# One core: Z records dealt unevenly over the points, one weight load moved ahead of a wait, and the mLSTM output projection as four block pairs

## The chip, the cores and the metric

The kernel runs on one core of one Trainium2 chip. The metric is the device time of one execution in microseconds. The engines are TensorE (PE; its weight loads, PEld, overlap its matmuls), VectorE (DVE), ScalarE (ACT), GpSimd (POOL) and SyncE (SP), which issues most transfers. Each engine works in order. Semaphores tie the programs together: `x.then_inc(s, n)` counts up when x ends, and `wait_ge(s, n)` holds an engine until the count is there.

## What is computed

One decoder layer over 1024 tokens of width 1024, in fp32. Two mixers read one projection of the normed input and are merged by gates:

```python
mod = jax.nn.silu(c) @ w_ada[l] + b_ada[l]
h = rms_norm(x, g_norm[l]) * (1.0 + scale) + shift
proj = h @ w_in[l]
xa, va, oa, za, ia, fa, qa, ka, vat, zb, ga, gb = jnp.split(proj, split_at, axis=-1)
xc = jax.nn.silu(causal_depthwise_conv(xa, w_conv[l], b_conv[l]))
h_m = mlstm_chunkwise(q_m, k_m, v_m, ia + b_igate[l], fa + b_fgate[l])   # 4 heads of 256
h_m = jax.nn.sigmoid(oa) * h_m
h_m = rms_norm(h_m, g_mlstm_head[l]) + skip_mlstm[l] * xc
y_m = (h_m * jax.nn.silu(za)) @ w_out_mlstm[l]                          # 1024 x 1024
...                                    # 3 groups x 4 heads of dilated window attention
o_a = jnp.sum(wts[..., None] * jnp.stack(outs, axis=0), axis=0)
y_a = (o_a * jax.nn.silu(zb)) @ w_out_attn[l]                           # 512 x 1024
merged = jax.nn.sigmoid(ga) * y_m + jax.nn.sigmoid(gb) * y_a
x = x + gate * (merged @ w_out[l])
return rms_norm(x, g_final)
```

Shapes and names are shortened here; the code above is the reference cut to its core.

## The kernel before

**Precision.** Every large product is formed in three passes on PE: an operand is split into a high part (an fp32r copy, mostly made by ACT) and a low part (the rest, by POOL or DVE as a subtraction), and `three_pass` issues high·high, low·high and high·low (lines L592, L593, L594). One such matmul of 128x512 is called a record below.

**Stages.** Setup; then 28 *block pairs*, in which four 512x512 blocks of the input projection are had from seven products instead of eight (`ORDER = (5, 1, 2, 4, 6, 7, 3)`, 12 records each), with sums of the factor blocks made once by DVE and sums of weight blocks made for each pair; then four mixed stages, one for each head; then `merge`; then `finish`.

**A head's stage.** PE forms the rest of the head's projection, and last its Z (two chunks ZA and ZA+1, two halves each, 24 records a half: 96 records). The Z records are dealt out over 24 *points*, four at each; between them `mixing(u)` issues what the two mixers have at point u: an mLSTM chunk (scores, numerator, state, turn) and attention tasks (scores, transposes of the exponentials, p·v). These small matmuls wait for DVE, ACT and POOL. ACT copies a finished half out of its bank (`keep`), makes high parts of the next weights (`next_high`), and at points 17 to 21 takes the roots for the norms. After the last point `turn_output` (L1366) transposes the normed and gated head. `turn_stats` on SP stores the head's gated rows `um` (`mlstm_branch`), loads the softmax statistics `ct`, waits for the group weights `cw` (semaphore `cw_done`), stores them and spreads them over partitions. SP loads the ring of weights `wraw` with `load`; the fourth load of the next head stands behind these waits.

**merge.** `first_pairs` projects the gates of output tiles 0 and 1 (8 units of 24 records; the weights of the second four are made high by `pair_high` on ACT and low by POOL in line L1248). Meanwhile SP loads all eight `um` tiles back, and DVE combines the last head's attention groups (`scale_two`, `join_two`, `join_third`, `gate_attn`). Then `branch` forms, for each of eight tiles m of 128 output channels, the mLSTM part (16 x 24 = 384 records in all) and the attention part (192 records), with weights loaded and split for each. DVE's `merge_tile(m)` multiplies both by their gates and adds them into `mg`; ACT stores the tile to DRAM (`mg_d`) as soon as it is merged. Tiles 2 to 7 do mLSTM then attention, alternately; the last two units of PE's work are mLSTM tile 7 and attention tile 7.

**finish.** POOL waits until tiles 0 to 6 are in DRAM, loads 128 tokens of all of them back (`wraw<-merged`), splits them (L2178, L2181), and only then can PE form the first output tile; tile 7 is taken from SBUF. PE forms 8 token tiles of the output projection, DVE and ACT the final norm.

The waits which set this order around the merge, in code:

```python
pool.wait_ge(mg_out, 16 * KT)                      # finish: tiles 0 to 6 stored
pool.dma_start(mr[:, b, 0:KT - 1], rows[:, 0:KT - 1, b * P:(b + 1) * P]).then_inc(m_in[b], 16)
pe.wait_ge(m_part, 1)                              # finish: first high and low parts are there
act.wait_ge(merged_half, 4 * m + 4)                # merge: tile m is merged
act.dma_start(mg_d[m], mg[:]).then_inc(mg_out, 16)
```

## Time and profile before

| | before |
|---|---|
| runs | 1370.96 us median of 3 (1369.63 to 1371.36) |
| profiled execution, its time | 1371.11 us |
| its span | 1369.3 us |
| mean granted clock of PE | 0.999 of full speed |
| PE busy | 1345.7 us (98%) |
| DVE, ACT, POOL busy | 855.3, 580.1, 463.0 us (62%, 42%, 34%) |
| chain that ended last | PE 87%, DVE 6%, ACT 3%, DMA 2% |

The span runs from the first to the last instruction on the engines; the time of the execution is 1.8 us more. Matmuls are pipelined, so a matmul's listed duration (389 ns for a record) is more than its share of PE's time: eight records that follow each other start 0.227 us apart. The stages in the trace, by their first matmuls: blocks to about 610, heads at 610, 734.3, 856, 976.5, merge 1097.8, its branch products 1141.4, output 1273.45, last matmul about 1363.

### The profile page before, as it was taken

How to read it: one execution, taken by the hardware profiler on the slowest of the kernel's cores; microseconds unless marked ns; L12 is line 12 of the kernel's file. 1: busy time of each engine (PE TensorE's matmuls, PEld its weight loads, DVE VectorE, ACT ScalarE, POOL GpSimd, SP SyncE). 2: the span in 40 equal slices, each digit the busy share in tenths (PEclk: the TensorE clock that was granted, in tenths of full speed). 3: DMA queues.
4: the chain of work that ended last, by engine and by line, in shares of the span. 5: the costliest groups of instructions: out<-in, count | busy, mean ns of one | idle time of the engine just before them, and what ended most of it. 6: DMA issues, size and time to landing. Idle time of an engine off the chain costs nothing.

```text
span 1369.3 us, 17469 instructions
## 1 busy us (share of the span) xinstructions
PE 1345.7 (98%) x6453; PEld 1126.9 (82%) x6453; DVE 855.3 (62%) x1472; ACT 580.1 (42%) x1016; POOL 463.0 (34%) x298
## 2 busy tenths in 40 slices
PE   8999999999999999999999999999999999999998
PEld 6888888888888888888898788889878887888886
DVE  7988766573745444535368757866875766434586
ACT  7663353343444344332545446354545534111122
POOL 0096555554545555543002200210120022222551
PEclk9999999999999999999999999999999999999999
DMA  8522323323234343337231841553172165453543
GB/s 316 196 82 95 132 99 123 123 93 115 101 123 139 123 143 134 139 112 228 73 83 48 231 93 32 161 148 94 48 227 67 33 241 205 128 187 140 173 138 108
DMA packets 65454, 180.52 MB, mean 132 GB/s; under 512 B 22001, under 2 KB 22129, under 8 KB 63318
## 3 DMA queue, kind: packets, MB, share of 16 engines
q1 hardware_dynamic: 61082, 166.64, 36.9%
q10 hardware_dynamic: 3168, 8.70, 1.9%
q0 software_dynamic: 1120, 4.06, 1.0%
q8 instruction: 52, 0.85, 0.3%
q14 instruction: 32, 0.26, 0.1%
HBM read 132.49 MB, written 46.89 MB: 131 GB/s over the span
## 4 chain that ended last, share of the span: by engine, by line
PE 87%; DVE 6%; ACT 3%; DMA 2%; issue 1%; SPq 0%; POOL 0%; ACTq 0%; DVEq 0%
PE banks L592 23%; PE banks L594 23%; PE banks L593 23%; PE banks L1265 4%; PE banks L1390 2%; PE banks L1400 2%; PE banks L1350 2%; PE banks L1356 2%; DMA wraw<-in_w_all 1%; PE banks L1339 1%; PE banks L1348 1%; PE banks L1409 1%; PE banks L584 1%; PE banks L556 1%; PE banks L1378 1%
## 5 line engine op out<-in xcount | busy, mean ns | idle before, releaser
L1248 POOL TENSOR_TENSOR wlo<-wraw,whi 128x1024 fp32r<-128x1024 f32 x28 | 72.1, 2575 | 436.5 <-ACT whi L1468 411.1
L718 POOL TENSOR_TENSOR wlo<-w_sum,whi 128x512 fp32r<-128x512 f32 x112 | 165.2, 1477 | 137.4 <-ACT whi L843 137.4
L592 PE MATMUL banks<-t_hi,whi 128*128 128x512 f32 x448 | 174.3, 389 | 0.0
L593 PE MATMUL banks<-t_lo,whi 128*128 128x512 f32 x448 | 174.3, 389 | 0.0
L594 PE MATMUL banks<-t_hi,wlo 128*128 128x512 f32 x448 | 174.3, 389 | 0.0
L989 DVE TENSOR_TENSOR c_sum<-c_sum,banks 128x512 f32<-128x512 f32 x196 | 134.4, 686 | 44.7 <-PE banks L594 30.6
L592 PE MATMUL banks<-h_hi,whi 128*128 128x512 f32 x416 | 162.0, 389 | 0.0
L594 PE MATMUL banks<-h_hi,wlo 128*128 128x512 f32 x416 | 161.9, 389 | 0.0
L593 PE MATMUL banks<-h_lo,whi 128*128 128x512 f32 x416 | 161.8, 389 | 0.0
L843 ACT ACTIVATE whi<-w_sum 128x512 fp32r<-128x512 f32 x112 | 70.5, 630 | 165.5 <-PE banks L594 100.7
L592 PE MATMUL banks<-whi,h_hi 128*128 128x512 f32 x256 | 100.2, 391 | 1.4 <-POOL wlo L1248 1.4
L594 PE MATMUL banks<-whi,h_lo 128*128 128x512 f32 x256 | 99.7, 389 | 0.0
L593 PE MATMUL banks<-wlo,h_hi 128*128 128x512 f32 x256 | 99.6, 389 | 0.0
L593 PEld LDWEIGHTS banks<-t_lo,whi 128*128 128x128 f32 x448 | 84.1, 188 | 17.5
L594 PEld LDWEIGHTS banks<-t_hi,wlo 128*128 128x128 f32 x448 | 84.1, 188 | 17.4
L592 PEld LDWEIGHTS banks<-t_hi,whi 128*128 128x128 f32 x448 | 84.1, 188 | 17.4
L592 PEld LDWEIGHTS banks<-h_hi,whi 128*128 128x128 f32 x416 | 78.1, 188 | 16.3 <-POOL wlo L1248 0.2
L594 PEld LDWEIGHTS banks<-h_hi,wlo 128*128 128x128 f32 x416 | 78.1, 188 | 16.3
L593 PEld LDWEIGHTS banks<-h_lo,whi 128*128 128x128 f32 x416 | 78.1, 188 | 16.2
L865 ACT ACTIVATE fin<-c_sum 128x1024 f32<-128x1024 f32 x56 | 79.4, 1467 | 2.4 <-DMA chunk_decay_rows<-wlast 2.3
L718 POOL TENSOR_TENSOR wlo<-wraw,whi 128x512 fp32r<-128x512 f32 x42 | 63.0, 1507 | 48.8 <-ACT whi L843 48.8
L718 POOL TENSOR_TENSOR wlo<-raw,whi 128x512 fp32r<-128x512 f32 x42 | 58.5, 1402 | 51.3 <-ACT whi L843 51.3
(374 smaller groups left out, 2904.8 us busy)
## 6 DMA issues: line engine op xcount, KB each, us to landing
wraw<-in_w_all SPq DMA_DIRECT2D x72, 512.0 KB, 4.3
raw<-in_w_all SPq DMA_DIRECT2D x28, 512.0 KB, 4.4
queries_keys<-fin SPq DMA_DIRECT2D x12, 1024.0 KB, 4.0
qa<-queries_keys SPq DMA_DIRECT2D x12, 768.0 KB, 13.7
s_wada<-in_w_ada_cols SPq DMA_DIRECT2D x16, 512.0 KB, 8.2
attn_values<-fin SPq DMA_DIRECT2D x6, 1024.0 KB, 4.0
tn<-attn_values SPq DMA_DIRECT2D x12, 512.0 KB, 10.1
sig_c<-merge_gates SPq DMA_DIRECT2D x6, 1024.0 KB, 6.4
```

The source lines that it names most:

```text
L592: t_.matmul(out, w_hi, x_hi, start=first, stop=False)
L593: t_.matmul(out, w_hi, x_lo, start=False, stop=False)
L594: return t_.matmul(out, w_lo, x_hi, start=False, stop=last)
L718: nc.gpsimd.tensor_tensor(wlo4[:, o % 4, :], source(r, j), whi4[:, o % 4, :].bitcast(F32), subtract).then_inc(s_split, 1)
L843: A(whi4[:, o % 4, :], source(r, j), ACT.Copy).then_inc(s_high, 1)
L865: A(fin[r % 2][:, j, :].rearrange("p (r u) -> p r u", r=d), c_sum[:, r % 2, j, :].rearrange("p (u r) -> p r u", r=d), ACT.Sigmoid if r < Q ...
L989: v.tensor_tensor(out, x, bank(r, j), ALU.add).then_inc(part_added, 1)
L1248: nc.gpsimd.tensor_tensor(to, wraw[:, q % 2, :], hi.bitcast(F32), ALU.subtract).then_inc(w_split, 1)
L1265: mm = t_.matmul(ps[:, h, :], w[:, to, k * P:(k + 1) * P], x[:, k, h * HALF:(h + 1) * HALF], start=(e == 0), stop=(e == 3 * KT - 1))
L1350: mm = t_.matmul(M2[:, 0:DH + 1], qm[:, d, c * P:(c + 1) * P], cst[:, d, :], start=(d == 0), stop=(d == 1))
L1356: mm = t_.matmul((M1, M2)[d][:, 0:DH + 1], kw[:, c % 2, d * P:(d + 1) * P], v1[:, c, 0:DH + 1], start=True, stop=True)
L1390: mm = t_.matmul(A0[:, u * 2 * P:u * 2 * P + b * P], qa[:, g % 2, 0, t * P:(t + 1) * P], qa[:, g % 2, 1, (t + 1 - b) * P:(t + 1) * P], sta ...
```

## The change

It has three parts.

1. **Heads.** The 96 Z records of a head are dealt out over the 24 points by the table `SIZES`: 4, 4, 6, 7, then twelve times 3, three times 4, then 7, 4, 4, 6, 6. ACT's `keep` and `next_high` move with the records: the second half is now finished at point 12 instead of 11, the third at point 19 (after the point's mixing) instead of 17.
2. **Weight load.** For heads 1 to 3 the fourth load of the ring is issued in `turn_stats` of the head before, after `ct` and before the wait for `cw_done`.
3. **Branch.** The mLSTM part of the merge is formed as four more block pairs, r = 28 to 31: 7 products of 12 records each, 336 instead of 384. The factor blocks are quarters of `um` (128x4x512 a piece); DVE makes four differences and seven low parts of them, ACT seven high parts. For each pair DVE makes four sums of weight blocks, ACT and POOL split seven, ACT keeps the first product, and DVE adds the others (`join`, seven additions) into `umo`, then multiplies two tiles by their gates. All eight attention tiles (8 x 24 records) follow after the four pairs. The rows of `um` for it are loaded by `gather_branch` on SP, ahead of `ct`; the last head's two come straight from SBUF. `weigh_groups` and `group_exp` of head 3 move from the end of the heads into the merge's programs. Gates come in halves, and the output weights in another order (`OUT_ORDER`). The wait of `finish` for the stored tiles 0 to 6 stays.

```diff
+    RECORDS = 3 * KT
+    SIZES = (4, 4, 6, 7) + 12 * (3,) + 3 * (4,) + (7, 4, 4, 6, 6)
+    ENDS = list(itertools.accumulate(SIZES))
+    POINTS = len(SIZES)
...
+        def gather_branch():
+            um_raw, tile_in = T["um_raw"], T["tile_in"]
+            sp.wait_ge(out_turned, 4 * HEADS)
+            for q in range(2):
+                sp.wait_ge(um_out[q], 16 * HEADS)
+            for k in range(KH):
+                sp.dma_start(um_raw[:, k, :], um_d[k // 2, k % 2]).then_inc(tile_in[k], 16)
+            for q in range(2):
+                sp.wait_ge(um_done, 2 * HEADS - 1 + q)
+                sp.dma_start(um_raw[:, KT - 2 + q, :], xc[:, q, :]).then_inc(tile_in[KT - 2 + q], 16)
...
-            for q in range(2):
+            if i == HEADS - 1:
+                gather_branch()
+            for q in range(2) if i < HEADS - 1 else ():
                 sp.wait_ge(um_done, i * 2 + q + 1)
                 sp.dma_start(um_d[i, q], xc[:, q, :]).then_inc(um_out[q], 16)
             sp.wait_ge(stat_out, (i + 1) * 16 * sum(STATS))
             sp.dma_start(ct[:].rearrange("p g c w -> p g (c w)"), stat_d.rearrange("g (p c) w -> p g (c w)", c=NCH)).then_inc(ct_in, 16)
+            for k in range(KH, KT - 2) if i == HEADS - 1 else ():
+                sp.dma_start(T["um_raw"][:, k, :], um_d[k // 2, k % 2]).then_inc(T["tile_in"][k], 16)
+            if i + 1 < HEADS:
+                load(HEAD0 + (i + 1) * CHUNKS + AHEAD)
             sp.wait_ge(cw_done, i + 1)
             sp.dma_start(coef_d.rearrange("g (p c) -> p g c", c=NCH), cw[:, 2]).then_inc(coef_out, 16)
...
-                load(HEAD0 + i * CHUNKS + p + AHEAD)
+                if p or not i:
+                    load(HEAD0 + i * CHUNKS + p + AHEAD)
...
+            for u in range(POINTS):
+                for record in range(ENDS[u] - SIZES[u], ENDS[u]):
+                    project(record)
+                if u == 1:
+                    head_q()
+                if (i, u) == (0, 2):
+                    pe.wait_ge(decays_in, 32)
+                    t_.transpose(M1[:, 0:P], gr[:], ident[:]).then_inc(hc_turned, 1)
+                mixing(u)
...
+            for u in range(POINTS):
+                if u == formed_at(ZA, 0):
+                    keep(ZA, 0)
+                if u == formed_at(ZA, 1):
+                    keep(ZA, 1)
+                    next_high(ZA + 2)
+                if u == formed_at(ZA + 1, 1):
+                    keep(ZA + 1, 1)
+                    next_high(ZA + 3)
+                if u == 1:
+                    exp_table()
...
+                    keep(ZA + 1, 0)
+                if u == TURN - 2:
...
+        load_pair(PAIRS)
         sp.wait_ge(T["ua_done"], 2 * HEADS + 1)
         sp.dma_start(ua_d[HEADS - 1], T["mixing"]["szb"][:]).then_inc(ua_out, 16)
+        load_pair(PAIRS + 1)
...
+        for r in BRANCH_PAIRS:
+            for j in ORDER:
+                o = at_product(r, j)
+                pool.wait_ge(s_high, o + 1)
+                nc.gpsimd.tensor_tensor(wlo4[:, o % 4, :], source(r, j), whi4[:, o % 4, :].bitcast(F32), ALU.subtract).then_inc(s_split, 1)
...
+        def product(r, j):
+            o = at_product(r, j)
+            bank_free(o)
+            pe.wait_ge(s_split, o + 1)
+            if r == PAIRS:
+                pe.wait_ge(t_lo_done, low_count(j))
+            hi, lo = factors[j]
+            for k in range(KH):
+                cols = slice(k * P, (k + 1) * P)
+                mm = three_pass(t_, bank(r, j), whi4[:, o % 4, cols], wlo4[:, o % 4, cols], hi[:, k, :], lo[:, k, :],
+                                k == 0, k == KH - 1)
+            mm.then_inc(gprod, 1)
...
+        for r in BRANCH_PAIRS:
+            for j in ORDER:
+                product(r, j)
+        for m in range(KT):
+            attn_branch(m)
...
+        def weight_high(o):
+            r, j = o // PRODUCTS, ORDER[o % PRODUCTS]
+            if o < TOTAL + 4:
+                act.wait_ge(proj, PROJ0 + 4 * PLAIN - (1 if o < TOTAL + 2 else 0))
+            else:
+                act.wait_ge(gprod, o - 3)
+            if j in plain_at:
+                act.wait_ge(pair_in[r % 2], 32 * (r // 2 + 1))
+            else:
+                act.wait_ge(s_added, made(r, j))
+            A(whi4[:, o % 4, :], source(r, j), ACT.Copy).then_inc(s_high, 1)
...
         act.sem_inc(mg_out, 16)
+        branch_high(up_left_hi, up_left[0], range(KH))
+        T["shared"]["group_exp"](HEADS - 1)
         first_sigmoid(0, 0, 1)
         first_sigmoid(0, 1, 1)
+        sum_high(5)
         pair_high(0)
         first_sigmoid(0, 0, 0)
         pair_high(1)
         first_sigmoid(0, 1, 0)
+        branch_high(low_left_hi, low_left[0], range(KH, KT))
         first_sigmoid(1, 0, 1)
-        split_high(0)
-        split_high(1)
         first_sigmoid(1, 1, 1)
-        split_high(2)
-        split_high(3)
-        branch_high(0)
+        weight_high(TOTAL)
+        weight_high(TOTAL + 1)
         first_sigmoid(1, 0, 0)
-        split_high(4)
-        split_high(5)
-        branch_high(1)
+        act.wait_ge(ua_out, 16 * HEADS + 16)
+        sum_high(6)
+        sum_high(4)
         first_sigmoid(1, 1, 0)
-        for k in range(EARLY, KB):
-            split_high(k)
-        branch_high(2)
-        for k in range(2):
-            out_high(k)
+        weight_high(TOTAL + 2)
+        weight_high(TOTAL + 3)
+        for o in range(TOTAL, WITH_BRANCH):
+            r, j = o // PRODUCTS, ORDER[o % PRODUCTS]
+            if j == 1:
+                keep_first(r)
+            if o + 4 < WITH_BRANCH:
+                weight_high(o + 4)
+            if o == TOTAL:
+                sum_high(7)
+            if o == TOTAL + 1:
+                branch_high(low_right_hi, low_right[0], range(KH, KT))
+        attn_weights_high(0)
+        for k in range(HEADS):
+            attn_high(k)
+        attn_weights_high(1)
         for m in range(KT):
-            for r in (2 * m + 3, 2 * m + 4):
-                if r < 2 * KT:
-                    branch_high(r)
-            act.wait_ge(merged_half, 4 * m + 4)
-            act.dma_start(mg_d[m], mg[:]).then_inc(mg_out, 16)
             if m + 2 < KT:
-                out_high(m + 2)
+                attn_weights_high(m + 2)
+            act.wait_ge(merged_half, merged(m, 4))
+            if m == KT - 1:
+                act.wait_ge(mg_out, 16 * KT)
+            act.dma_start(mg_d[m], umo[:, m, :]).then_inc(mg_out, 16)
+            if m < len(WO_AT):
+                for e in WO_AT[m]:
+                    out_high(e)
...
+        def difference(j, x, y, first=None):
+            if first is not None:
+                dve.wait_ge(t_raw, raw_count(first))
+            v.tensor_tensor(bt_raw[j], x, y, ALU.subtract).then_inc(t_raw, 1)
...
+        def low(j, raw_):
+            hi, lo = factors[j]
+            dve.wait_ge(t_hi_done, high_count(j))
+            v.tensor_tensor(lo, raw_, f(hi), ALU.subtract).then_inc(t_lo_done, 1)
...
+        def weight_sums(r):
+            dve.wait_ge(pair_in[r % 2], 32 * (r // 2 + 1))
+            dve.wait_ge(s_split, PRODUCTS * r)
+            combine(5, quarter(r, 1, 0), quarter(r, 1, 1), ALU.add)
+            combine(7, quarter(r, 0, 0), quarter(r, 1, 0), ALU.subtract)
+            dve.wait_ge(s_added, made(r, 5))
+            combine(6, sum_at[5], quarter(r, 0, 0), ALU.subtract)
+            dve.wait_ge(s_added, made(r, 6))
+            combine(3, quarter(r, 0, 1), sum_at[6], ALU.subtract)
...
         dve.sem_inc(T["added"], 4)
-        T["shared"]["scale_two"](HEADS - 1)
-        T["shared"]["join_two"](HEADS - 1)
-        T["shared"]["join_third"](HEADS - 1)
-        T["shared"]["gate_attn"](HEADS - 1)
-        for k in range(KB):
-            split_low(k)
-        for k in range(2):
-            out_low(k)
+        branch_rows(range(KH))
+        dve.wait_ge(pv_kept, 12 * HEADS + 1)
+        difference(5, up_right, up_left[0])
+        T["shared"]["weigh_groups"](HEADS - 1)
+        low(1, up_left[0])
+        branch_rows(range(KH, KT))
+        difference(6, low_right[0], bt_raw[5], 5)
+        low(5, bt_raw[5])
+        for part in ("scale_two", "join_two", "join_third", "gate_attn"):
+            T["shared"][part](HEADS - 1)
+        dve.wait_ge(T["ua_done"], 2 * HEADS + 1)
+        weight_sums(PAIRS)
+        difference(4, low_left[0], bt_raw[6], 6)
+        low(2, low_left[0])
+        low(4, bt_raw[4])
+        low(6, bt_raw[6])
+        difference(7, low_right[0], up_right)
+        low(7, bt_raw[7])
+        low(3, low_right[0])
+        for r in BRANCH_PAIRS:
+            if r + 1 in BRANCH_PAIRS:
+                weight_sums(r + 1)
+            else:
+                for k in range(HEADS):
+                    attn_low(k)
+            join(r)
+            for j in range(2):
+                gate(2 * (r - PAIRS) + j)
         for m in range(KT):
             merge_tile(m)
-            if m + 2 < KT:
-                out_low(m + 2)
+            if m < len(WO_AT):
+                for e in WO_AT[m]:
+                    out_low(e)
```

**PE, the last points of head 3**, before: `pT,vt` is p·v of an attention task, `ident,sm` a transpose of exponentials, L1265 a Z record.

```order
L1390 MATMUL banks<-qa 128x128 x2
L1400 MATMUL banks<-pT,vt 128x128 x2
L1409 MATMUL banks<-ident,sm 128x128 x2
L1265 MATMUL banks<-h_lo,whi 128x512
L1265 MATMUL banks<-h_hi,wlo 128x512
L1265 MATMUL banks<-h_hi,whi 128x512
L1265 MATMUL banks<-h_lo,whi 128x512
L1400 MATMUL banks<-pT,vt 128x128 x2
L1409 MATMUL banks<-ident,sm 128x128 x2
```

PE, the same place in the changed kernel (L1308 is a Z record):

```order
L1433 MATMUL banks<-qa 128x128 x2
L1443 MATMUL banks<-pT,vt 128x128 x2
L1452 MATMUL banks<-ident,sm 128x128 x2
L1308 MATMUL banks<-h_hi,whi 128x512
L1308 MATMUL banks<-h_lo,whi 128x512
L1308 MATMUL banks<-h_hi,wlo 128x512
L1308 MATMUL banks<-h_hi,whi 128x512
L1308 MATMUL banks<-h_lo,whi 128x512
L1308 MATMUL banks<-h_hi,wlo 128x512
L1308 MATMUL banks<-h_hi,whi 128x512
L1443 MATMUL banks<-pT,vt 128x128 x2
L1452 MATMUL banks<-ident,sm 128x128 x2
```

Between one transpose of exponentials and the next attention product there are now seven records at point 19, where there were four.

**SP, from the last store of statistics to the merge**, before: `mlstm_branch` is the DRAM home of `um`, `ct` the statistics, `group_weights` the spread weights.

```order
L1176 DMA softmax_stats<-st 512x1x2
L1149 DMA wraw<-in_w_all 128x1024 [waits w_split]
L1182 DMA mlstm_branch<-xc 128x1024 [waits um_done] x2
L1184 DMA ct<-softmax_stats 128x3x16 [waits stat_out]
L1186 DMA group_weights<-cw 128x3x8 [waits cw_done]
L1193 DMA qm<-group_weights 128x1024 [waits coef_out]
L1193 DMA qm<-group_weights 128x1024
L1193 DMA vt<-group_weights 128x1024 [waits pv_kept]
L1936 DMA um_lo_raw<-mlstm_branch 128x1024 [waits p_kept,pv_kept,masked,um_out0,out_used,um_out1,acc_out,early_out]
L1936 DMA um_lo_raw<-mlstm_branch 128x1024 x7
L1919 DMA wraw<-in_w_all 128x1024 [waits w_split] x2
```

SP, the same place in the changed kernel:

```order
L1173 DMA wraw<-in_w_all 128x1024 [waits w_split]
L1208 DMA um_lo_raw<-mlstm_branch 128x1024 [waits um_out1,um_out0,out_turned]
L1208 DMA um_lo_raw<-mlstm_branch 128x1024 x3
L1211 DMA um_lo_raw<-xc 128x1024 [waits um_done] x2
L1221 DMA ct<-softmax_stats 128x3x16 [waits stat_out]
L1223 DMA um_lo_raw<-mlstm_branch 128x1024 x2
L1227 DMA group_weights<-cw 128x3x8 [waits cw_done]
L1234 DMA qm<-group_weights 128x1024 [waits coef_out]
L1234 DMA qm<-group_weights 128x1024
L1234 DMA vt<-group_weights 128x1024 [waits pv_kept]
L1986 DMA wraw<-in_w_all 128x1024 [waits w_split,acc_out,early_out]
L1986 DMA wraw<-in_w_all 128x1024
```

The loads of `um` now stand ahead of `ct` and of the wait for `cw_done`; the weights of the first two block pairs follow behind the spreads, and `w_split` of the second gate pair stands before them.

**ACT, the start of the merge**, before: L2021 is a sigmoid of a finished gate unit, L2027 `pair_high`.

```order
L1545 ACT_TABLE_LOAD
L1545 ACTIVATE cw<-cw 128x24 [waits ct_arg]
L2021 ACT_TABLE_LOAD
L2021 ACTIVATE qa<-banks 128x512 [waits proj] x2
L2027 ACTIVATE whi<-wraw 128x1024 [waits w_in0,proj]
L2021 ACTIVATE qa<-banks 128x512 [waits proj]
L2027 ACTIVATE whi<-wraw 128x1024 [waits w_in1,proj]
L2021 ACTIVATE qa<-banks 128x512 [waits proj] x2
```

ACT, the same place in the changed kernel (L2143 the sigmoids, L2149 `pair_high`, L2155 and L2160 high parts of factor blocks):

```order
L2155 ACTIVATE up_left_hi<-um_lo_raw 128x2048 [waits tile_in2,tile_in3,tile_in1,tile_in0]
L1587 ACT_TABLE_LOAD
L1587 ACTIVATE cw<-cw 128x24 [waits ct_arg]
L2143 ACT_TABLE_LOAD
L2143 ACTIVATE qa<-banks 128x512 [waits proj] x2
L2160 ACTIVATE bt_hi<-bt_lo_raw 128x2048 [waits t_raw]
L2149 ACTIVATE whi<-wraw 128x1024 [waits w_in0,proj]
L2143 ACTIVATE qa<-banks 128x512 [waits proj]
L2149 ACTIVATE whi<-wraw 128x1024 [waits w_in1,proj]
L2143 ACTIVATE qa<-banks 128x512 [waits proj]
L2155 ACTIVATE low_left_hi<-um_lo_raw 128x2048 [waits tile_in6,tile_in7,tile_in5,tile_in4]
L2143 ACTIVATE qa<-banks 128x512 [waits proj] x2
```

Ahead of the first `pair_high` there now stand the high part of a block of `um`, the exponential of the group weights with its table, and the high part of the first difference.

## Rows read from the trace of the kernel before

**Rows 1.** Waits of PE: line that waited, releaser, total us, times, longest

```profile
PE banks L1366 <- DVE og L1719: 2.2, 4, 0.6
...
PE banks L1400 <- ACT ew L1565: 1.8, 4, 0.4
PE banks L592 <- POOL wlo L1248: 1.4, 2, 1.0
...
PE banks L592 <- DVE um_lo L2085: 0.8, 2, 0.6
```

**Rows 2.** Windows by stage: length, busy us and count of each engine, clock, DMA share

```profile
1097.80:1141.40 43.60, 43.60 (x195) 35.99 (x194) 28.84 (x29) 16.86 (x21) 11.17 (x4) 1.00 0.63 230
...
1273.45:1369.30 95.85, 89.28 (x413) 74.03 (x411) 66.96 (x111) 20.59 (x51) 37.95 (x23) 0.98 0.39 127
```

**Rows 3.** Timeline of SP and ACT around head 3's fourth weight load

```profile
998.60 1.19 SPq L1149 DMA_DIRECT2D wraw<-in_w_all  x2
...
1006.44 1.06 ACT L1468 ACTIVATE whi<-wraw 128x1024 fp32r<-128x1024 f32 x1 [3.09 <-DMA wraw<-in_w_all]
```

**Rows 4.** Timeline of ACT and PE at point 4 of head 3

```profile
1037.18 0.19 ACT L1570 ACTIVATION_READ_ACCUMULATOR sm<-sm,nm 128x1 f32 x1
...
1037.46 0.51 PE L1409 MATMUL banks<-ident,sm 128*128 128x128 f32 x3
```

**Rows 5.** Page, transfers: KB each, median us to landing; SP's timeline, start of merge

```profile
wraw<-in_w_all SPq DMA_DIRECT2D x72, 512.0 KB, 4.3
...
1100.84 0.35 SPq L1149 DMA_DIRECT2D wraw<-in_w_all  x1
```

**Rows 6.** Timeline of ACT, POOL and DVE in the merge's gate units

```profile
1108.24 1.28 ACT L2021 ACT_TABLE_LOAD   x1
...
1114.45 1.06 ACT L2027 ACTIVATE whi<-wraw 128x1024 fp32r<-128x1024 f32 x1 [3.83 <-PE banks L594]
...
1115.59 2.39 POOL L1248 TENSOR_TENSOR wlo<-wraw,whi 128x1024 fp32r<-128x1024 f32 x1 [14.77 <-ACT whi L2027]
...
1119.47 3.25 DVE L1787 TENSOR_TENSOR num<-num,qm 128x1024 f32<-128x1024 f32 x2 [10.17 <-DMA vt<-group_weights]
...
1132.14 2.35 DVE L2085 TENSOR_TENSOR um_lo<-um_lo_raw,um_hi_a 128x1024 fp32r<-128x1024 f32 x2
```

**Rows 7.** Timeline of DVE and POOL in setup, and of POOL in the blocks

```profile
57.50 2.35 DVE L919 TENSOR_TENSOR t_lo_raw<-s_xnT 128x1024 f32<-128x1024 f32 x2
59.88 4.58 DVE L919 TENSOR_TENSOR t_lo_raw<-s_xnT,t_lo_raw 128x1024 f32<-128x1024 f32 x2
...
59.83 2.41 POOL L723 TENSOR_TENSOR wlo<-wraw,whi 128x1024 fp32r<-128x1024 f32 x1 [56.88 <-ACT whi L875]
...
299.49 1.29 POOL L718 TENSOR_TENSOR wlo<-w_sum,whi 128x512 fp32r<-128x512 f32 x1 [0.88 <-ACT whi L843]
```

**Rows 8.** Timeline of DVE, ACT and POOL from merged tile 6 to the output

```profile
1259.91 0.69 DVE L2108 TENSOR_TENSOR num<-num,sig_c 128x512 f32<-128x512 f32 x1
...
1260.63 15.58 ACTq L2074 DMA_DIRECT2D merged<-num  x2
...
1263.58 2.10 POOL L2187 DMA_DIRECT2D wraw<-merged  x2 [3.88 <-DMA merged<-num]
1268.23 1.67 POOL L2178 TENSOR_TENSOR m_first<-wraw,zero 128x896 fp32r<-128x896 f32 x1 [2.54 <-DMA wraw<-merged]
1269.98 2.13 POOL L2181 TENSOR_TENSOR m_first<-wraw,m_first 128x896 fp32r<-128x896 f32 x1
```

**Rows 9.** Windows after the last matmul and around PE's first dense work

```profile
1362.00:1365.00 3.00, 0.73 (x7) 0.52 (x5) 1.68 (x6) 0.71 (x3) 0.00 (x0) 1.00 0.00 0
...
1366.00:1369.30 3.30, 0.00 (x0) 0.00 (x0) 0.10 (x1) 0.33 (x1) 0.00 (x0) 0.50 0.42 159
10.80:14.00 3.20, 3.20 (x16) 3.20 (x16) 2.69 (x6) 1.93 (x2) 0.00 (x0) 1.00 1.01 412
14.00:15.60 1.60, 1.60 (x17) 1.60 (x16) 0.83 (x6) 1.28 (x4) 0.00 (x0) 1.00 1.02 412
```

435 lines of the change are left out of this document (257 added, 178 removed).

## The prediction

> **What bounds the kernel now.** I read the page's busy table first: PE is busy 1345.7 of 1369.3 us at a clock of 0.999, so this kernel is the row of its matmuls and the few places where that row stops. The page gives both. Then the waits of PE [rows 1], which name those stops: four short ones ahead of L1366 (the turn of a head's output), four ahead of L1400 (p·v at point 18), two ahead of L592 for low weight parts, two for low parts of `um`. Then windows by stage [rows 2]: the gate units take 43.60 us for 192 records, so a record costs 43.60 / 192 = 0.227 us of PE, whatever its listed duration says. Then the timelines of the other engines at the places where the change puts work. There the reader is to ask what stands between two engines and how much PE work covers it.
>
> **What it removes.**
> 1. 48 records of the branch (384 to 336): 48 x 0.227 = -10.9 us. No other engine ends the stretch there, so PE's time goes in full.
> 2. The two waits for `um_lo`: -0.8 [rows 1]. Those tiles are gone; the new factor parts are priced below.
> 3. L1366: 2.2 us in 4 waits, 0.55 a head [rows 1]. The numerator whose normed value it waits for comes at point 18. From there to the turn there were 20 records (4 before each of points 19 to 23), now 7 + 4 + 4 + 6 + 6 = 27. Seven more are 1.6 us, over 0.55: -2.2.
> 4. L1400: 1.8 us in 4, 0.45 each [rows 1]. It waits for ACT's weight L1565, queued behind the norm's square. The 7 records ahead of point 19 in place of 4 are 0.68 us of cover against 0.45: -1.8.
> 5. The low weights L1248: 1.4 us in 2 waits, 1.0 the longest [rows 1]. Of head 3, SP issues the load of this slot at 998.60, behind the group weights and their spreads, and ACT stands 3.09 us idle for it before its high part at 1006.44 [rows 3]. Issued ahead of the `cw_done` wait it is earlier by several us: -1.4.
>
> Sum of what goes: 10.9 + 0.8 + 2.2 + 1.8 + 1.4 = 17.1 us.
>
> **What the heads pay.** The twelve points with three records have one record less between a task's scores and the use of its exponentials. At point 4 of head 3 ACT's exponential ends at 1037.18 + 0.19 = 1037.37 and PE takes it at 1037.46 [rows 4]: 0.09 us in hand, and a record is 0.227, so a new wait of about 0.14 us there. Most other points have more in hand; I take 0.25 a head, +1.0. Bounds: nothing, if DVE's earlier start gives it back, and all 12 points exposed in 4 heads, 48 x 0.227 = +10.9.
>
> **The first pair's factors: the gate units.** Today the high part of the second gate weights starts at 1114.45 and ends at 1115.51, and POOL splits it from 1115.59 to 1117.98 [rows 6]. PE needs it after four units, at 1097.80 + 4 x 24 x 0.227 = 1119.6: 1.6 us in hand. With the wait at L1366 gone PE comes there at 1119.0. In the new ACT program five things stand ahead: the high part of the first four `um` tiles, the exponential with its table, the sigmoid's table, two sigmoids, and the high part of the first difference, which DVE must form first. When do the tiles land? SP is through with the last ring load at 1100.84; that load and four tiles are 5 x 0.52 = 2.6 MB, at the 412 GB/s which the queues move in a full stretch [rows 9] 6.4 us, plus what one such load takes beyond its own 1.3 us of transfer, 4.3 - 1.3 = 3.0 [rows 5]: 1110.2. DVE's difference is two 128x1024 pieces, 2.35 us [rows 7], to 1112.6; the group weights then take 0.5. ACT's parts are four tables or copies: after 1113.1 a sigmoid table of 1.28 [rows 6] and the exponential 0.2, two sigmoids 1.1, a copy of 128x2048 2.0 (two of the 1.06 copies, less their overlap) and `pair_high` 1.06: 1118.8. The exponential's own table, 1.28, can load only after the first copy, 1110.2 + 2.0 + 1.3 = 1113.5, which moves this to 1119.1. POOL's 2.39 makes it 1121.5 against 1119.0: **+2.4** us of wait. It is us for us with the landing: at the best case (tiles 2.4 us sooner) nothing.
>
> **The first pair's factors: the products.** DVE's attention chain runs from 1119.47 to 1132.2 today, when the spreads have landed [rows 6]. The statistics now stand behind six tiles, so I move it by 4 to 5 us, to about 1136. Behind it stand four weight sums (0.7 each) and, until product 3, two differences and five low parts, each 2.35 us. A product is 12 records, 2.72 us, and five of the seven products of this pair (2, 4, 6, 7, 3) need one or two such DVE steps: 2, 4, 6 and 3 one, 7 two, and one more difference ahead of 2. Alone DVE would just hold: 2.35 against 2.72. But POOL splits a weight block in each product, 1.29 us alone [rows 7], and the two do not run beside each other here: from 59.88 two DVE subtractions of 2.35 took 4.58 us, with a POOL subtraction of 2.41 lying at 59.83 [rows 7]; 2.35 + 2.41 = 4.76. So a product in this pair takes 2.35 + 1.29 = 3.64 us, 0.92 more than 2.72. Over six products 5.5 us. Some splits fall in DVE's own waits for ACT, so I take **+4.0**; bounds 0 and 5.5. The Trainium skill (page "SBUF — State Buffer", section "SBUF: two separate sides") says that a VectorE operation with two inputs in SBUF and a GpSimd operation that reads SBUF hold a shared port pair in turn, the loser blocked for the whole instruction. By that rule it would be the full 5.5, by the naive reading of separate engines nothing. Rows 7 agree with the rule.
>
> In pairs 29 to 31 DVE has sums 2.8, joins 4.8 (banks) and gates 2.4 us in 19.0, POOL 9.0; that fits, as in the 28 pairs before, where PE has no wait for either.
>
> **The output: what becomes visible.** Follow merged tile 6 today [rows 8]: DVE's last addition ends at 1260.60, ACT issues the store at 1260.63, POOL is released at 1263.58, its load is back at 1268.23, its two subtractions (1.67, 2.13) end at 1272.11. 11.5 us, and the output starts at 1273.45 [rows 2]: it all lay under mLSTM tile 7 and attention tile 7, 72 records or 16.3 us. In the new order only attention tile 7 follows attention tile 6: 24 records, 5.44 us. Tile 6 is merged 4 x 0.69 less the overlap with its own second half, about 1.7 us, after its last record; so 5.44 - 1.7 = 3.7 us before PE's end, and the chain needs 11.5: **+7.8** us in which PE has nothing to do. Bounds: 7.0, and 10 if DVE is late with tile 6 (eight output-weight low parts stand between the tiles).
>
> **The clock.** PE idles 7.8 us. The last matmuls are over by about 1363; the granted clock is 1.00 in 1362 to 1365 and 0.50, the 1.2 GHz level, from 1366 on [rows 9]. So it will be down when the output starts. No row shows a rise of the granted clock. The nearest is PE's pace in its first dense work: 16 matmuls in the 3.2 us from 10.8 and 17 of the same in the next 1.6 us, though the clock column says 1.00 for both [rows 9]. If that is what a rise looks like, half of 3.2 us is lost: **+1.6** (bounds 0, if the clock stays up, and 3.2, twice the stretch). The Trainium skill ("TensorE: Matmul & The Clock Gate", table "The two states you'll see") has the same two levels, 1.2 GHz after idling and 2.4 GHz after sustained work. The trace agrees for the fall; that the chip starts low is its reading of the first stretch, which the column doesn't show.
>
> **Sum**, against the profiled execution's own 1371.1 us (span 1369.3 and 1.8 around it), which is 0.15 over the median of the three runs: 1371.1 - 17.1 + 1.0 + 2.4 + 4.0 + 7.8 + 1.6 = **1370.8 us**, the median's own size: no difference.
>
> **The rivals.**
> - *The factor steps keep ahead* (0.25). The tiles land 2.4 us sooner, as transfers of head 3 are out of the way, and POOL's splits fall into DVE's gaps: 1370.8 - 2.4 - 4.0 = 1364.4. For it: DVE is idle 10.17 us before 1119.47 [rows 6]. Against: rows 7.
> - *The output's chain is partly covered, or the clock stays up* (0.10). If only half of the 7.8 shows and the clock holds, 1370.8 - 3.9 - 1.6 = 1365.3. Against: nothing but one 5.44 us unit is left behind tile 6.
> - *Slower: the gather lands late* (0.15). `pair_high` is chained to the landing us for us. The 4.7 MB of all tiles, statistics and last load share the queues; if the first four tiles come 4 us later than 1110.2, the wait is 6.4 and the attention chain and everything behind it moves too: 1374.8. It decides (slower by over 0.2%) from 3 us late.
> - *Slower: short points exposed* (0.10). If the 48 shortened points each show their record, 1370.8 - 1.0 + 10.9 = 1380.7; a third of them is enough for slower. For it: 0.09 us in hand in rows 4. Against: one point of twelve was that tight.
> - *The heads' part does nothing* (0.05), since other waits end at the same time: 5.4 - 1.0 back, 1375.2.
> - My forecast as it stands, 1368.2 to 1373.7: 0.35.
>
> **How the numbers follow.** A measurement of this kernel tells apart about 0.2%, 2.7 us: faster is under 1368.2, slower over 1373.7. Faster: the first two rivals, 0.35. Same: 0.37, the forecast and 0.02 of mild cases of the rivals. Slower: 0.28. The range leaves out the exposed points and the far end of the first two: 1363.5 to 1376.0; the likeliest case's own range is 1368 to 1374.
>
> **What would show it.** In the profile after: no wait at L1366's and L1400's successors, and none for the low weights in the heads; a wait of 2 to 3 us of PE on POOL's low weights at the fifth gate unit; in the first branch pair waits of about 0.9 us on DVE's low parts, product by product, with POOL splits of over 1.5 us; then pairs without waits; an idle stretch of PE of 7 to 9 us before the first output matmul, ended by POOL's split; and 1.2 GHz in the 3 us after it. What would make it wrong: DVE late in the attention tiles, so that the idle stretch is over 10 us; or output weights that land after tile 4, so that ACT holds up the attention weights.

## The result: 1.5% slower

The changed kernel takes 1392.45 us (median of 4 runs, 1383.21 to 1395.48) against 1371.16 us before (4 runs): ratio 1.0146, 95% interval 1.0097 to 1.0194. The forecast was 1370.8, the range ended at 1376.0. Its profiled execution took 1393.01 us (span 1391.2), 21.9 more than that of before. The edges of the stages in the two traces, by their first matmuls, say where:

| stretch | before | after | difference | forecast |
|---|---|---|---|---|
| start to the first folded projection | 662.1 | 663.7 | +1.6 | 0 |
| four heads, to the last turn | 433.7 | 441.6 | +7.9 | -4.4 |
| last turn to the first output matmul | 177.6 | 187.3 | +9.6 | +2.5 |
| first output matmul to the end | 95.9 | 98.6 | +2.8 | +1.6 |

The folded projection is the first product of a head with `fold` as an operand, and a turn is the first matmul of L1366 (L1409 after). The first row is no part of the change, but it is part of the time: in setup, which has the same work in both kernels, the granted clock fell in this execution and not in that of before. The same window of both (length, busy us and count of PE, PEld, DVE, ACT, POOL, granted clock, DMA share, GB/s), first before, then after:

```profile
28.50:32.00 3.50, 3.50 (x21) 2.80 (x21) 3.36 (x7) 3.43 (x4) 0.00 (x0) 1.00 0.81 234
28.50:32.00 3.50, 3.50 (x14) 3.02 (x13) 3.42 (x7) 3.43 (x4) 0.00 (x0) 0.51 1.00 343
```

That is 3.4 us at half the clock, 1.7 us lost. The last stop of PE ahead of it was 0.5 us (at 26), in both kernels. Of the 14 profiled executions of this text nine have this fall and begin their first folded projection at 662.8 to 664.1, and five (before, e3, e4, e6 and e8) do not and begin it at 661.7 to 662.1.

The four runs of the changed kernel spread over 12 us, and the mean granted clock goes with them: 1383.21 us at 0.994, 1391.89 at 0.990, 1393.01 and 1395.48 at 0.986. What follows is read from the 1393.01 us, near the median; the shortest of the four shows that not all of the loss comes in every execution. The kernel before had medians of 1371.16, 1370.06, 1370.26 and 1370.36 us beside the result, e1 to e4, e5 to e8 and e9 to e12, so differences between runs of different sets are good to about 1 us.

PE's waits in the changed kernel, by line, releaser, total us, times, longest:

```profile
PE banks L614 <- POOL m_first L2407: 7.8, 1, 7.8
PE banks L1443 <- DVE pT L1810: 7.6, 4, 1.9
...
PE banks L614 <- POOL wlo L2060: 3.5, 1, 3.5
...
PE banks L614 <- POOL wlo L1290: 2.6, 1, 2.6
...
PE banks L614 <- POOL wlo L2056: 1.5, 2, 1.3
```

The waits of [rows 1] are gone, all four kinds, as forecast. New are: 7.8 ahead of the output (forecast 7.8), 2.6 at the gate units (2.4), 1.5 in the first pair under a name and more in pieces (below). And two that no sum had: 7.6 us at L1443 in four waits of 1.9, in the heads, and 3.5 at L2060, in the attention tiles.

**The wait in the heads.** ACT, DVE, POOL and PE in head 4 around point 12:

```profile
1073.09 0.57 ACT L1494 ACTIVATE cv<-banks 128x512 f32<-128x512 f32 x1
1073.57 1.04 ACT L1510 ACTIVATE whi<-wraw 128x1024 fp32r<-128x1024 f32 x1
1074.51 0.46 ACT L1578 ACTIVATE hin<-banks,hc 128x257 f32<-128x257 f32 x1
...
1074.69 2.37 POOL L1290 TENSOR_TENSOR wlo<-wraw,whi 128x1024 fp32r<-128x1024 f32 x1 [39.09 <-ACT whi L1510]
...
1075.01 0.43 DVE L1734 TENSOR_TENSOR hnb<-banks,hin 128x257 f32<-128x257 f32 x1 [2.32 <-ACT hin L1578]
...
1075.66 1.42 DVE L1741 SCALAR_TENSOR_TENSOR small<-hnb,hc,small 128x1 f32<-128x1 f32 x1
...
1078.52 0.62 DVE L1810 COPY pT<-banks 128x128 f32<-128x128 f32 x2
...
1079.19 1.02 PE L1443 MATMUL banks<-pT,vt 128*128 128x128 f32 x6 [1.90 <-DVE pT L1810]
```

ACT copies the finished half out of its bank (L1494) and makes the next weights high (L1510, 1.04 us) before the mLSTM's state term (L1578). DVE stands 2.32 us for that term (1.22 in e1 below, where the copies come later). Then an operation on one column, L1741, takes 1.42 us, and ends with POOL's split of those same weights (POOL is busy 1074.69 to 1077.06). In the kernel before, the same operation took 0.22 us all 32 times. The transposed exponentials (L1810) come last, and PE waits for them. So the two copies hold up PE in two ways: in ACT's own queue, and through the split that they release on POOL. Before the change, they stood at point 11, and PE's longest wait at p·v was 0.4 us [rows 1].

**And the clock falls.** Windows of the changed kernel, in one-microsecond steps behind that wait:

```profile
1079.00:1080.00 1.00, 0.81 (x6) 0.81 (x7) 1.00 (x4) 1.00 (x6) 0.00 (x0) 0.95 0.99 373
1080.00:1081.00 1.00, 1.00 (x6) 0.98 (x5) 0.62 (x3) 0.41 (x2) 0.00 (x0) 0.50 0.98 401
...
1082.00:1083.00 1.00, 1.00 (x4) 0.81 (x3) 0.00 (x0) 0.00 (x0) 0.00 (x0) 0.50 0.16 2
1083.00:1084.00 1.00, 1.00 (x5) 0.82 (x5) 0.00 (x0) 0.00 (x0) 0.00 (x0) 0.84 0.02 0
```

PE is up to full work again at 1079.2, and from 1079.9 to about 1083.3 it is granted 0.50, the 1.2 GHz level: 3.4 us at half the clock, 1.7 us lost. So a stop of 1.9 us costs about 3.6 here. It is so in all four heads of this execution. The sum closes: from folded projection to turn a head takes 73.0 us where it took 70.3, 2.7 more, which is 1.9 + 1.7 less the 0.95 of the two short waits that are gone.

**The merge's start**, where [rows 6] are of before: ACT, POOL and PE at the second gate weights:

```profile
1120.49 1.92 ACT L2155 ACTIVATE up_left_hi<-um_lo_raw 128x2048 fp32r<-128x2048 f32 x1 [11.45 <-DMA um_lo_raw<-mlstm_branch]
...
1128.29 1.06 ACT L2149 ACTIVATE whi<-wraw 128x1024 fp32r<-128x1024 f32 x1
...
1129.43 6.86 POOL L1290 TENSOR_TENSOR wlo<-wraw,whi 128x1024 fp32r<-128x1024 f32 x2 [18.86 <-ACT whi L2149]
...
1131.94 0.50 PE L614 MATMUL banks<-h_hi,whi 128*128 128x512 f32 x1 [2.64 <-POOL wlo L1290]
```

The first four tiles of `um` land at 1120.5, 9.9 us behind the last ring load (1110.59); 9.4 were forecast. ACT's high part of the gate weights ends at 1129.35 behind its queue, and PE stands 2.64 us.

**The attention tiles.** SP, ACT and PE at tile 5:

```profile
1257.65 0.33 SPq L2007 DMA_DIRECT2D gate<-merge_gates  x1
1258.02 0.43 SPq L1994 DMA_DIRECT2D wraw<-in_w_all  x1
...
1263.40 0.63 ACT L2183 ACTIVATE whi<-wraw 128x512 fp32r<-128x512 f32 x1 [3.33 <-DMA wraw<-in_w_all]
...
1265.43 0.80 PE L614 MATMUL banks<-ua_hi_a,whi 128*128 128x512 f32 x1 [3.50 <-POOL wlo L2060]
```

The weights of tile 5 are issued at 1258.02, directly behind a gate load (1257.65) that had to wait until tile 2 was merged, land 5.4 us later, and PE, done with tile 4 at 1261.9, waits 3.5 us. The clock follows here too, and stays at 0.50 until about 1271.0 (a mean of 0.90 over the second window is one microsecond at 0.50):

```profile
1265.00:1270.00 5.00, 4.57 (x11) 3.61 (x12) 3.80 (x5) 0.78 (x2) 0.37 (x1) 0.50 0.76 262
1270.00:1275.00 5.00, 5.00 (x21) 4.05 (x20) 3.45 (x5) 1.45 (x2) 1.29 (x1) 0.90 0.77 231
```

**The output.** POOL's load and subtractions, and the windows of the first output matmuls:

```profile
1283.74 2.10 POOL L2413 DMA_DIRECT2D wraw<-merged  x2 [5.65 <-DMA merged<-umo]
1288.70 1.67 POOL L2404 TENSOR_TENSOR m_first<-wraw,zero 128x896 fp32r<-128x896 f32 x1 [2.86 <-DMA wraw<-merged]
1290.45 2.07 POOL L2407 TENSOR_TENSOR m_first<-wraw,m_first 128x896 fp32r<-128x896 f32 x1
...
1285.00:1290.00 5.00, 0.00 (x0) 0.00 (x0) 1.23 (x2) 0.00 (x0) 2.14 (x2) 0.81 0.89 260
1290.00:1295.00 5.00, 2.43 (x6) 1.97 (x7) 0.00 (x0) 0.00 (x0) 3.43 (x6) 0.50 1.00 379
1295.00:1300.00 5.00, 5.00 (x17) 3.98 (x16) 0.00 (x0) 0.00 (x0) 4.68 (x5) 0.66 0.43 175
1300.00:1305.00 5.00, 5.00 (x20) 3.44 (x19) 2.12 (x3) 0.00 (x0) 0.78 (x1) 1.00 0.35 105
```

This is the chain of [rows 8], link by link, now in the open: load 1283.74, parts 1288.70 and 1290.45, first output matmul at 1292.57, where PE's last branch matmul ended at 1284.8. Tile 6 was merged 4.1 us before that (3.7 were forecast), and from there the chain took 11.8 us (11.5 before). The clock is at 0.50 until about 1298.3, 5.8 us after PE has resumed: half of that is 2.9 us, and the output stage is 2.8 us longer.

### The profile page after: what moved, and what is told of

It reads as the page before. It is cut to its first block, busy times and chain, and to the rows that moved or that the text cites. A ratio compares the mean times of both kernels' runs of the same rounds, so it can differ in the third digit from the quotient of the medians.

```text
span 1391.2 us, 17535 instructions
## 1 busy us (share of the span) xinstructions
PE 1350.2 (97%) x6405; PEld 1128.3 (81%) x6405; DVE 913.2 (66%) x1511; ACT 595.2 (43%) x1039; POOL 501.0 (36%) x318
## 4 chain that ended last, share of the span: by engine, by line
PE 79%; DVE 9%; ACT 4%; POOL 3%; DMA 3%; issue 1%; SPq 0%; ACTq 0%; DVEq 0%; POOLq 0%
PE banks L614 21%; PE banks L616 21%; PE banks L615 20%; PE banks L1308 5%; PE banks L1443 2%; POOL wlo L739 2%; PE banks L1433 2%; PE banks L1393 1%; PE banks L1399 1%; PE banks L1391 1%; PE banks L1452 1%; PE banks L578 1%; DMA wraw<-in_w_all 1%; DVE bt_lo L2259 1%; PE banks L1421 1%
## 5 line engine op out<-in xcount | busy, mean ns | idle before, releaser
L1290 POOL TENSOR_TENSOR wlo<-wraw,whi 128x1024 fp32r<-128x1024 f32 x28 | 75.0, 2681 | 440.6 <-ACT whi L1510 414.1
```

What stands on the lines that cost most here:

```text
L1290: nc.gpsimd.tensor_tensor(to, wraw[:, q % 2, :], hi.bitcast(F32), ALU.subtract).then_inc(w_split, 1)
```

## The experiments

Theory after the result: (1) in the heads it is ACT's two copies, moved from point 11 to point 12, and not the number of records; (2) a stop of PE of about 2 us or more can be followed by a fall of the clock, and that costs 1.7 to 2.9 us besides; (3) the attention wait is SP's order; (4) the output's wait is the round trip through DRAM. The rivals stand in the expectations. e1 serves as the base of e5 to e9, e11 and e12.

**e1, the copies behind point 12.**

```diff
-                if u == formed_at(ZA, 1):
-                    keep(ZA, 1)
-                    next_high(ZA + 2)
...
                 mixing(u)
+                if u == formed_at(ZA, 1):
+                    keep(ZA, 1)
+                    next_high(ZA + 2)
```

> The changed kernel, with ACT's keep of the second Z half and the copy of the next weights issued behind mixing(12) and not ahead of it. Theory: these two (0.57 and 1.04 us) hold up ACT's state term at point 12, DVE stands 2.3 us for it, PE 1.9 us for p transposed (L1443), four times, and each such stop lets PE's granted clock fall to 0.50 for some 4 us, about 1.7 us more. Then both go: 4 x 3.7 = 15 us less, about 1378 us, no window under 1.00 in the heads. Rival (three records in place of four are too little cover at any point, wherever ACT's copies stand): the four waits of 1.9 us stay, 1392 us.

Measured 1376.93 us (4 runs), 1.0054 of before (1.0039 to 1.0069), 15.5 less than the changed kernel. No wait at L1443 is left:

```profile
PE banks L614 <- POOL m_first L2407: 7.1, 1, 7.1
...
PE banks L614 <- POOL wlo L2060: 4.1, 2, 3.8
PE banks L614 <- POOL wlo L2056: 3.8, 1, 3.8
...
PE banks L614 <- POOL wlo L1290: 2.5, 1, 2.5
```

From the first folded projection to the last turn there are now 426.1 us, 7.7 less than before the change, where 4.4 were forecast. Of the 7.7, 4.9 us lie between folded projection and turn, in the part with the points, and 2.8 between a turn and the next folded projection, where part 2 works (e4's profile has 2.2 there). The edit moves the copies and with them POOL's split (L1741 takes at most 0.22 us in e1), so it does not tell ACT's queue and POOL's split apart.

**e2, even deal; e3, part 1 alone; e4, part 2 alone.** e2 is the changed kernel with four records at each point:

```diff
-    SIZES = (4, 4, 6, 7) + 12 * (3,) + 3 * (4,) + (7, 4, 4, 6, 6)
+    SIZES = 24 * (4,)
...
+                if u == formed_at(ZA + 1, 0):
+                    keep(ZA + 1, 0)
...
                 mixing(u)
-                if u == formed_at(ZA + 1, 0):
-                    keep(ZA + 1, 0)
```

> The changed kernel with four Z records at each point and ACT's keeps where the kernel before has them (part 1 undone; parts 2 and 3 stay). Theory: each head's stretch from its folded projection to its turn comes back from 73.0 to 70.3 us, so about 10 us less than the changed kernel, 1382 us, with the short waits at L1443 and at the turn (0.4 and 0.6 us a head) back. Rival (part 2 or 3 lengthens the heads): 1392 us.

e3 is the kernel before with the diff's hunks on `SIZES`, PE's and ACT's loops over the points. e4 is the kernel before with

```diff
+            if i + 1 < HEADS:
+                load(HEAD0 + (i + 1) * CHUNKS + AHEAD)
             sp.wait_ge(cw_done, i + 1)
...
-                load(HEAD0 + i * CHUNKS + p + AHEAD)
+                if p or not i:
+                    load(HEAD0 + i * CHUNKS + p + AHEAD)
```

> The kernel before with part 1 alone (table SIZES and ACT's keeps as in the change). Theory: the loss in the heads is part 1's own: 4 x 2.7 = 11 us more than before, about 1382 us, with the waits of 1.9 us at p.v and the clock at 0.50 behind each. Rival (it takes parts 2 or 3 to make it): within 3 us of 1371, or 4 us less as forecast.

> The kernel before with part 2 alone (fourth weight load ahead of the wait for cw_done). Forecast of the prediction: the two waits of PE on low weights L1248 (1.4 us) go, 1369.6 us; rival: the load was no cause, another wait takes their place, 1371 us.

| | median us | ratio to before, 95% |
|---|---|---|
| e2 | 1381.55 (4 runs) | 1.0084 (1.0068 to 1.0099) |
| e3 | 1376.77 (4 runs) | 1.0059 (1.0041 to 1.0077) |
| e4 | 1368.61 (10 runs) | 0.9990 (0.9980 to 0.9999) |

e2 met its number: part 1 as it was made costs 11 us beside an even deal. e3 has the four waits of 1.9 us, but is 5 us under its expectation, and its trace offers a reason. Windows of six microseconds behind the wait, first and second head of e3:

```profile
708.00:714.00 6.00, 5.34 (x25) 4.69 (x25) 2.60 (x9) 2.18 (x8) 0.00 (x0) 0.72 0.52 159
832.00:838.00 6.00, 5.70 (x35) 5.17 (x36) 3.85 (x13) 2.67 (x10) 0.00 (x0) 1.00 0.51 154
```

The same wait, the same instructions; behind the first the clock falls (mean 0.72, 25 matmuls), behind the second it stays (35). From folded projection to turn the first head takes 73.1 us, the others 71.3. The fall costs 1.8 us by these edges (1.7 by its 3.4 us at 0.50), and whether one comes at a stop of 1.9 us differs; three falls less would make the 5 us. What decides it was not settled. e4: PE's waits for L1248 are gone and the time is 1.45 us lower at the medians, of which the interval says only that it is between 0.1 and 2.7.

**e5 to e8, the four costs of the branch, one at a time**, each on e1.

e5, the first output blocks from SBUF (`umo` holds all merged tiles):

```diff
-        pool.wait_ge(mg_out, 16 * KT)
-        pool.wait_ge(T["bw_split"], KT)
-        for b in range(2):
-            pool.dma_start(mr[:, b, 0:KT - 1], rows[:, 0:KT - 1, b * P:(b + 1) * P]).then_inc(m_in[b], 16)
-        pool.wait_ge(m_in[0], 16)
+        umo = T["umo"]
         pool.wait_ge(merged_half, merged(KT - 1, 0))
-        split(0, slice(0, KT - 1), mr[:, 0, 0:KT - 1], 1).then_inc(m_part, 1)
+        split(0, slice(0, KT - 1), umo[:, 0:KT - 1, 0:P], 1).then_inc(m_part, 1)
...
```

The second output block is changed in the same way.

> As e1_keep_late, but the first two output token blocks take the merged tiles 0 to 6 from the buffer in SBUF where they were merged, in place of the store to DRAM and the load back. Theory: PE's idle of 7.1 us ahead of the output is that chain, only two POOL subtractions (3.8 us) are left of it behind merged tile 6, so the idle falls under 1 us and the clock does not fall: 7 us and some 2 us of clock less, about 1368 us. Rival (another wait ends there at the same time: gates, output weights): the idle stays over 4 us.

Measured 1368.95 us (10 runs), 8.0 under e1; 0.9992 of before (0.9983 to 1.0002). The idle ahead of the output is gone altogether; in its place stands a smaller one, inside the output's first block, for a row loaded late. The clock, which was expected to stay up, falls behind this one too (0.50 from 1278 to 1281, 1.7 us lost):

```profile
PE banks L614 <- POOL wlo L2060: 3.6, 1, 3.6
...
PE banks L2435 <- DMA gf<-in_g_final: 2.3, 1, 2.3
```

e6, the order of SP's loads and DVE's low parts in the attention tiles:

```diff
+        load_attn_weights(4)
         for m in range(2, KT):
-            if m + 2 < KT:
-                load_attn_weights(m + 2)
+            if m + 3 < KT:
+                load_attn_weights(m + 3)
...
             merge_tile(m)
-            if m < len(WO_AT):
-                for e in WO_AT[m]:
+            if 0 < m <= len(WO_AT):
+                for e in WO_AT[m - 1]:
                     out_low(e)
```

> As e1_keep_late, but SP issues the attention weights of tile m+3 ahead of the late gate of tile m+2, and DVE makes output-weight low parts behind the next tile's merge. Theory: the wait of PE on the weights of attention tile 5 (3.8 us) is SP's: their load stood behind a gate load that waits for merged tile 2. It goes, with the clock's fall behind it: 4.1 + 1.7 = 6 us less, 1371 us. Rival (DVE's 6.9 us a tile is the bound, not the load): a wait stays at tile 5 to 7, 2 us less at most.

Measured 1368.83 us (10 runs), 8.1 under e1; 0.9990 (0.9981 to 0.9999). No wait for L2060's line is left. The two edits were made together, so which of them did it was not tried. The gain is 8 where 6 were expected. Two things in the profiles bear on this and are no part of the edit: PE's longest wait in the first pair is 1.0 us in e6 and 3.8 in e1 (the clock fell behind it), and e1 has the fall in setup that e6 has not. Against that, e6 has a fall behind its wait of 2.6 us at the gate units, and e1 has none. How much of the medians' 8.1 is the edit's own stays open.

e7, PE kept busy in the idle stretch:

```diff
+        pe.wait_ge(merged_half, merged(KT - 2, 0))
+        pe.wait_ge(b_lo_done, HEADS + 1)
+        for _ in range(34):
+            nc.tensor.matmul(ps[:, 5, :], T["kept_on"]["whi"][:, 0, 0:P], wo[4][0][:, 0:HALF], start=True, stop=True)
         pe.wait_ge(m_part, 1)
```

> As e1_keep_late, with 34 matmuls of 128x512 into an unused bank in PE's idle stretch ahead of the output (7.7 us of work in 7.1 us of idle and the store's margin). Theory: the idle stretch costs its own length and a fall of the clock on top; with PE busy the clock stays at 1.00 and the output runs at full pace from its start: 1 to 2.5 us less than e1, 1375 us. Rival (the clock costs nothing there): the same or 0.6 us more, 1377.5.

Inconclusive. In the profiled execution, 1374.82 us, it went as the theory has it: the clock stays at full speed through the first output matmuls (the first is at 1277.06), and from there to the end there are 95.9 us, where e1 has 98.0:

```profile
1275.00:1280.00 5.00, 3.78 (x17) 2.82 (x16) 0.00 (x0) 0.00 (x0) 4.66 (x5) 1.00 1.03 412
1280.00:1285.00 5.00, 5.00 (x20) 3.48 (x19) 0.38 (x1) 0.00 (x0) 3.85 (x4) 1.00 0.16 56
```

But of its 9 runs three are at 1373.1 to 1374.8 and six at 1380.1 to 1383.3, above all of e1's (1375.7 to 1379.9). What the longer six lose was not profiled; four of them have a mean granted clock of 0.992, the three short ones 0.995 to 0.998.

e8, the second gate weights first:

```diff
         T["shared"]["group_exp"](HEADS - 1)
+        pair_high(0)
         first_sigmoid(0, 0, 1)
         first_sigmoid(0, 1, 1)
         sum_high(5)
-        pair_high(0)
```

> As e1_keep_late, with the high part of the second gate weights on ACT ahead of the first two sigmoids and of the high part of the first difference. Theory: ACT's queue (3 us of it) makes the wait of 2.5 us on POOL's low weights at the fifth gate unit; it goes, and DVE's chain is 1 us later: 1375 us. Rival (the landing of the um rows sets it all): the wait stays over 2 us, 1377 us.

1376.23 us (4 runs), 1.0053 (1.0033 to 1.0073): within 0.7 of e1, so the time decides for neither expectation. The wait at the gate units fell from 2.5 to 0.9 as the theory says, but it moved into the first pair, and the output's grew:

```profile
PE banks L614 <- POOL m_first L2407: 9.2, 1, 9.2
...
PE banks L614 <- issue: 2.3, 2, 1.9
...
PE banks L614 <- POOL wlo L2056: 1.0, 2, 0.8
PE banks L614 <- POOL wlo L1290: 0.9, 1, 0.9
```

PE stands 1.95 us at 1142.4, ahead of the third product. Its weights were split late: ACT's copy of them (1139.13) stood behind the high part of a difference which DVE ended 33.1 us after the first tiles of `um` had landed, and 32.1 after it in e1. The clock fell behind this stop as well. So the two costs look like one chain, where taking one only shows the other.

**e9, POOL out of the first pair.**

```diff
-                nc.gpsimd.tensor_tensor(wlo4[:, o % 4, :], source(r, j), whi4[:, o % 4, :].bitcast(F32), ALU.subtract).then_inc(s_split, 1)
+                n = 8 if r == PAIRS else HALF
+                nc.gpsimd.tensor_tensor(wlo4[:, o % 4, 0:n], source(r, j)[:, 0:n], whi4[:, o % 4, 0:n].bitcast(F32), ALU.subtract).then_inc(s_split, 1)
```

This kernel leaves out the low parts of the first pair's weights, all but 8 columns of 512.

> As e1_keep_late, but POOL's seven weight splits of the first branch pair are cut to 8 of their 512 columns; that pair's low weight parts are left out with it. Theory: DVE's subtractions of two SBUF operands and POOL's splits exclude each other, which makes each of them 3.3 us beside the other in that pair. Alone the DVE steps of 128x2048 take 2.3 us, and PE's waits of 1.1 to 3.9 us in that pair fall under 0.5 in all. Rival (DVE is slowed by transfers or by ACT): they stay at 3.3 us and the waits stay.

1373.82 us (8 runs), 3.1 under e1. DVE in the first pair, in e1, and below it in e9:

```profile
1137.13 3.38 DVE L2259 TENSOR_TENSOR um_lo<-um_lo_raw,low_left_hi 128x2048 fp32r<-128x2048 f32 x1
1140.43 6.68 DVE L2259 TENSOR_TENSOR bt_lo<-bt_lo_raw,bt_hi 128x2048 fp32r<-128x2048 f32 x2
1147.04 3.37 DVE L2254 TENSOR_TENSOR bt_lo_raw<-um_lo_raw 128x2048 f32<-128x2048 f32 x1
```

```profile
1136.40 2.29 DVE L2260 TENSOR_TENSOR um_lo<-um_lo_raw,low_left_hi 128x2048 fp32r<-128x2048 f32 x1
1140.43 4.50 DVE L2260 TENSOR_TENSOR bt_lo<-bt_lo_raw,bt_hi 128x2048 fp32r<-128x2048 f32 x2 [1.74 <-ACT bt_hi L2161]
1144.85 2.29 DVE L2255 TENSOR_TENSOR bt_lo_raw<-um_lo_raw 128x2048 f32<-128x2048 f32 x1
```

3.38, 6.68 for two and 3.37 us become 2.29, 4.50 and 2.29, with the same operands, ACT parts and transfers, and PE has no wait left in that pair. The theory holds: the prediction's 2.35 + 1.29 = 3.64 us for a DVE step and a split in turn is 3.3 to 3.4 here.

**e10 to e12, the good parts together.** e10 is the kernel before with parts 1 and 2 and e1's edit. e11 is e1 with the edits of e5 and e6, and the two constant rows ahead of SP's waits:

```diff
-        sp.wait_ge(proj, BRANCH_DONE)
+        sp.dma_start(bg[:], a["b_gate"].broadcast_to([P, D])).then_inc(row_in, 16)
+        sp.dma_start(gf[:], a["g_final"].broadcast_to([P, D])).then_inc(row_in, 16)
         sp.wait_ge(merged_half, merged(KT - 1, 0))
         sp.dma_start(gate[:], acc_d).then_inc(row_in, 16)
-        sp.dma_start(bg[:], a["b_gate"].broadcast_to([P, D])).then_inc(row_in, 16)
-        sp.dma_start(gf[:], a["g_final"].broadcast_to([P, D])).then_inc(row_in, 16)
```

e12 is e11 with no stores of merged tiles at all, every output block split from `umo`.

> The kernel before with parts 1 and 2 and ACT's two copies behind point 12; the branch as before. In e1 the heads take 7.7 us less than before between the first folded projection and the last turn, so 1370.3 - 7.7 = 1362.6 us. Rival (the gain is given back at the merge, where the gate weights or the um rows then are late): 1366 us or more.

> e1_keep_late with both edits of e5 and e6, and with the rows of gate bias and final gain loaded when the pairs are done instead of behind PE's last branch matmul. Theory: the gains add: 1376.9 - 8 - 8 = 1361 us, and the 2.3 us wait of e5 on the final gain's row goes too, 1358.5 us. Rival (the two edits paid for the same clock): 1363 us or more.

> e11_all_fixed with every output token block taken from the merged tiles in SBUF: no stores of merged tiles and no loads back. Theory: those transfers are hidden behind PE by now, so the same as e11 within 1 us. Rival (they slow POOL's splits and the loads of weights): 2 us less or more.

| | median us (4 runs each) | ratio to before, 95% |
|---|---|---|
| e10 | 1364.35 | 0.9950 (0.9934 to 0.9967) |
| e11 | 1360.54 | 0.9925 (0.9911 to 0.9940) |
| e12 | 1360.57 | 0.9925 (0.9910 to 0.9939) |

e10 is 1.8 us over its number, but nothing of the heads' gain is given back at the merge, as its rival has it: in its profile the heads take 426.1 us, the merge 177.6 and the output stage 95.8, the last two as before. What is over lies at the start, where the clock fell in setup (first folded projection at 663.8 against 662.1). e11 beats both kernels, 9.8 us under before and 31.9 under the changed one. Its forecast was 2 us lower. That forecast added the gains of e5 and e6, and in their profiles both have the same shorter wait in the first pair beside e1 (1.0 against 3.8), which would count it twice; the medians do not show whether it does. The waits of the merge's start are still there:

```profile
PE banks L614 <- POOL wlo L1290: 3.0, 1, 3.0
...
PE banks L614 <- POOL wlo L2057: 1.4, 2, 1.2
```

e12, equal to e11 within 0.1 us, shows that the round trips were hidden everywhere but at the first block. Its profile again has a single wait of 3.8 us in the first pair, as e1's, where e11 has 1.3 at most; what decides between the two was not settled. The four block pairs, once their longest waits are mended, are worth 1364.35 - 1360.54 = 3.8 us.

## Why the prediction was wrong

Point by point.

- **Removed work**: right for the records. A pair without long waits, the second, takes 19.2 us for its 84 records, 0.228 each, so 48 fewer are worth the 10.9. All four kinds of waits are gone. Part 2 was forecast at 1.4 us; e4's medians have 1.45 with a wide interval, and its heads are 2.2 us shorter in the trace.
- **What the heads pay: the step that failed.** The prediction said "I take 0.25 a head, +1.0" and looked for the price in the records: a point with three instead of four, at a place where 0.09 us was in hand [rows 4]. It did not price ACT's two copies, which the same table moved from point 11 to point 12, ahead of the state term that DVE waits for, nor POOL's split behind them. Measured: 1.9 us of PE and 1.7 of clock a head, 14.4 in all; e1, which moves only the copies, is 15.5 us faster. With the copies out of the way the shortened points show no wait of PE: 426.1 us, 7.7 less than before, where 4.4 was forecast. The rival "short points exposed" had the right stage and a size of 10.9, for the wrong reason.
- **Gate units**, +2.4: the wait is 2.6, the stretch 2.9 longer (46.55 us against 43.60).
- **The first pair**, +4.0: it takes 22.95 us against 19.2 of the second, 3.8 more. The waits that the profile names in it are 2.4 of that; the rest is in smaller gaps between its products. Mechanism shown by e9. That the sum hit so closely is partly luck: the same program text of that pair had waits of 1.5 us in all in e5 and e6 and of 3.8 in e1 and e12.
- **Attention tiles: left out of the sum.** The prediction named late output weights and ACT only as what could make it wrong. It was SP: a load behind a load that waits. 3.5 us, and the clock down for 5.6 us of work behind it, 2.8 more. e6 removes it, with SP's order and DVE's changed at once.
- **The output**, +7.8: 7.8, and link by link as worked out (4.1 us of cover against 3.7, a chain of 11.8 against 11.5). Shown by e5, which removes it.
- **The clock**, +1.6 for one fall: the term was mis-sized and its count was wrong. The stretch at 0.50 behind the output's idle was 5.8 us, so 2.9, within the bounds given. And seven falls came where one was forecast: one in setup and four in the heads at 1.7, one in the attention tiles at 2.8 and one at the output at 2.9: 14.2 us in all.

The heads' sum was wrong by 12.3 us, that of the merge by 7.1 (6.3 in the attention tiles, 0.5 at the gate units, 0.3 not placed), the output's clock by 1.2; with 1.6 at the start this makes the 22.2 us between 1370.8 and the profiled 1393.0.

## What to carry to other kernels

A table that deals out PE's work moves also what other engines hang on "when this half is done"; list these riders and see what stands behind each on its own engine. Where PE is 98% busy, a stop costs more than its length when the clock follows it (1.9 us became 3.6), so a price for a stop needs a term for the clock with a chance, and runs of one kernel that spread by several us are to be compared by their granted clock too. And when an order of work is turned round (here all mLSTM tiles, then all attention tiles), follow every chain that was hidden by the old neighbour: the last tile's store and load back kept every link (11.8 us against 11.5) and 7.8 of them came into the open.

## What was unexpected of the hardware

- A stop of PE of 1.9 us can be followed by a granted clock of 0.50 for 3.4 us (four times in the changed kernel) or by none (three of four heads of e3), in the same code. At the gate units, stops of 2.1 to 3.1 us were followed by a fall in e2, e5, e6, e7 and e9, and not in the changed kernel, e1, e11 and e12. Behind every stop of 3.5 us or more in the merge the clock fell.
- In setup the clock fell in nine of 14 profiled executions, near 28.5 us; the longest stop of PE in the 10 us ahead was 0.5 us.
- After a fall PE worked 2.9 us (the output in e2) to 5.8 us (the output in the changed kernel) at 0.50, and lost half of that.
- Beside each other, a DVE subtraction of 128x2048 and a POOL split of 128x512 took 3.3 to 3.4 us each, where they take 2.3 and 1.3 alone. An operation of DVE on a single column took 1.42 us beside a POOL split, and 0.22 without.
